# Combining expert outputs at the end of a mixture-of-experts stage: a selection product for the last expert, and the gathers of the others placed in the last round

## The chip, the cores and the metric

One core of a Trainium2 chip runs the whole program. The metric is the device time of one execution in microseconds. Three runs of the kernel before gave 1581.63, 1583.05 and 1589.31 us; their median is 1583.05 us.

## What is computed

The reference is a two-layer decoder over 512 tokens of width 1024. Layer 0 mixes tokens by an RWKV-7 recurrence, layer 1 by dilated window attention. Each layer ends with the same hierarchical mixture of experts: the router picks one of 4 groups and two of the 4 experts inside it, and the token's output is the weighted sum of the two:

```
gate = (one_hot(grp)[:, :, None] * within[:, None, :] * p_grp[:, :, None]).reshape(n_tok, 16)
y = zeros_like(t)
for e in range(16):
    hdn = silu(t @ w_gate[e]) * (t @ w_up[e])      # (1024 x 512) twice
    y = y + gate[:, e:e + 1] * (hdn @ w_down[e])   # (512 x 1024)
h = h + y
```

So only two of the 16 terms of a token differ from zero. A final RMS norm follows after layer 1.

## The kernel before

The stage is `moe(nc, io, g, layer)`, called once for each layer. P is 128 partitions, J = 4 is the number of tiles of 128 tokens, T = 512, D = 1024, NE = 16. The residual `h` is resident in SBUF as 128 x 4 x 1024. The stage does not multiply all tokens by all experts. Each expert has 128 places; a token of expert e with position `posf` there is in row 128 e + `posf` of that expert's block.

**Prologue.** VectorE (DVE) computes the router's choices, the weights `wgt` (one for each of the two choices), the position `posf` of every token within its expert, the list of tokens of each expert (`idx`) and, for each token and choice, the row of the DRAM buffer `out_dram` where its output will stand (`pos`). These are some 60 small DVE instructions, most of which wait for the one before (`Chain.link`). The last two write `most` and `mosti`, the length of the longest list (L1821, L1822). All 16 x 128 rows of `out_dram` that these places use are filled with zeros once, in the layer-0 mixing stage (L748).

**Rounds.** There is one round for each expert; the first and the last are written out, the 14 between are a hardware loop on each engine (`rounds`). SyncE loads each expert's three weight matrices in six 1 MB pieces (L1429). ScalarE (ACT) rounds each piece to a high part (L1435), DVE subtracts for the low part (L1439, or in two halves at L1830), and TensorE (PE) multiplies in three passes (L1446 to L1448). In round e, PE does gate half 0, the transposes of the hidden values of expert e-1 (`pe_hidden`, L1467), gate half 1, both halves of the down product of e-1, the transposes of the tokens of e+1 (`pe_tokens`, L1458), and both halves of up. ACT copies the two halves of the down product from PSUM to the one tile `yo` (L1527). After the last round (`moe` from `rounds(pe, round_)` on) PE still has the transposes and the down product of expert 15. DVE there does: the product gate x up (`dve_up`, L1509), one and a half of the last two splits, the low part of the hidden values (`dve_hidden`, L1519), and the other half split.

**GpSimd (POOL)** gathers the tokens of an expert (L1614, L1619) and stores its output: `store_output` copies a column of row numbers (L1530), waits for both halves of `yo`, issues an indirect DMA to `out_dram` (L1534), waits until it has landed and only then frees `yo`.

**End.** POOL waits for the last of the 16 stores, then issues 8 indirect gathers (L1651), for each token tile j its first and its second choice, 512 KB each, into the tiles `xn` and `xnT`. Between the wait and the gathers it makes four checks whether a list is longer than 128 (`overflow`, `no_overflow`: a value is loaded from SBUF to a register, then a branch). With such a list there would be further rounds. Only DVE adds: for each j it waits for both gathers of that tile, then makes two additions `h += wgt * row` of 128 x 1024 (L1878), each of which waits for the one before. ACT squares each finished tile of `h` for the next norm (`square_tile`, L63). Then all engines meet at a barrier (L96) and the next stage begins: attention after layer 0, the final norm and the store of the result after layer 1.

## Time and profile before

| | |
|---|---|
| median of three runs | 1583.05 us (1581.63 to 1589.31) |
| the profiled execution, own time | 1583.01 us |
| its span, first to last instruction | 1581.3 us |
| mean granted TensorE clock | 0.93 |
| busy: PE, PEld, DVE, ACT, POOL | 1360.4, 1066.0, 1006.1, 845.0, 373.4 us |
| expert stage of layer 0 | about 520 to 877 us in the span |
| expert stage of layer 1 | about 1213 to 1570 us |

Busy shares are means over stages with different limits. In the rounds PE is busy nearly all of the time; at the end of each expert stage it is not. Times in the timelines are microseconds from the start of the span, then the duration; the bracket at the end of a row gives how long the engine had been idle and what it waited for ("issue" is a time for which the profile names no releaser).

### The profile page before, as it was taken

How to read it: one execution, taken by the hardware profiler on the slowest of the kernel's cores; microseconds unless marked ns; L12 is line 12 of the kernel's file. 1: busy time of each engine (PE TensorE's matmuls, PEld its weight loads, DVE VectorE, ACT ScalarE, POOL GpSimd, SP SyncE). 2: the span in 40 equal slices, each digit the busy share in tenths (PEclk: the TensorE clock that was granted, in tenths of full speed). 3: DMA queues.
4: the chain of work that ended last, by engine and by line, in shares of the span. 5: the costliest groups of instructions: out<-in, count | busy, mean ns of one | idle time of the engine just before them, and what ended most of it. 6: DMA issues, size and time to landing. Idle time of an engine off the chain costs nothing. (4 is left out here: it accounts for less than half of the span.)

```text
span 1581.3 us, 29588 instructions
## 1 busy us (share of the span) xinstructions
PE 1360.4 (86%) x11579; PEld 1066.0 (67%) x11579; DVE 1006.1 (64%) x1316; ACT 845.0 (53%) x1255; POOL 373.4 (24%) x417
## 2 busy tenths in 40 slices
PE   4999996767689799999993599999988899999980
PEld 2276685657554678787882487778776778787860
DVE  5626752455643599989982435765444798989963
ACT  6535542434421378888881324444542488888851
POOL 1112153436440022332222100001110122332202
PEclk8999897998999799999996799999968899999995
DMA  5042300052442699999983331212102799999944
GB/s 167 20 140 80 133 1 15 16 153 84 136 149 94 221 347 380 379 384 382 379 325 115 115 121 55 80 54 80 54 1 89 285 379 383 383 385 376 377 165 167
DMA packets 172329, 302.46 MB, mean 191 GB/s; under 512 B 34720, under 2 KB 45088, under 8 KB 172224
## 3 DMA queue, kind: packets, MB, share of 16 engines
q1 hardware_dynamic: 159648, 271.59, 48.3%
q0 software_dynamic: 11520, 25.19, 4.3%
q10 hardware_dynamic: 1056, 4.19, 0.6%
q8 instruction: 76, 1.25, 0.3%
q14 instruction: 29, 0.24, 0.0%
HBM read 279.96 MB, written 35.65 MB: 200 GB/s over the span
## 5 line engine op out<-in xcount | busy, mean ns | idle before, releaser
L1439 DVE TENSOR_TENSOR moe_wlo<-moe_raw,moe_whi 128x2048 fp32r<-128x2048 f32 x160 | 365.4, 2287 | 36.4 <-ACT moe_whi L1435 32.0
L1435 ACT ACTIVATE moe_whi<-moe_raw 128x2048 fp32r<-128x2048 f32 x192 | 366.8, 1916 | 23.6 <-PE all_bank L1448 22.3
L1446 PE MATMUL all_bank<-moe_whi,moe_xhi 128*128 128x512 f32 x512 | 206.8, 404 | 4.1 <-DVE moe_xlo L1495 4.1
L1448 PE MATMUL all_bank<-moe_whi,moe_xlo 128*128 128x512 f32 x512 | 199.7, 390 | 0.0
L1447 PE MATMUL all_bank<-moe_wlo,moe_xhi 128*128 128x512 f32 x512 | 199.7, 390 | 0.0
L1446 PEld LDWEIGHTS all_bank<-moe_whi,moe_xhi 128*128 128x128 f32 x512 | 96.0, 187 | 26.7 <-DVE moe_xlo L1495 4.4
L1448 PEld LDWEIGHTS all_bank<-moe_whi,moe_xlo 128*128 128x128 f32 x512 | 96.1, 188 | 21.1
L1447 PEld LDWEIGHTS all_bank<-moe_wlo,moe_xhi 128*128 128x128 f32 x512 | 96.2, 188 | 18.1
L1446 PE MATMUL all_bank<-moe_whi,moe_hhi 128*128 128x512 f32 x256 | 101.9, 398 | 7.4 <-DVE moe_hlo L1519 7.4
L1611 POOL COPY moe_idxcol<-moe_idx 128x1 int32 (+1 forms) x30 | 34.5, 1150 | 310.9 <-PE all_bank L1458 310.9
L1447 PE MATMUL all_bank<-moe_wlo,moe_hhi 128*128 128x512 f32 x256 | 101.2, 395 | 0.0
L1448 PE MATMUL all_bank<-moe_whi,moe_hlo 128*128 128x512 f32 x256 | 101.1, 395 | 0.0
L2048 DVE SCALAR_TENSOR_TENSOR attn_wlo<-attn_xhat,all_par,attn_whi 128x512 fp32r<-128x512 f32 x64 | 43.8, 746 | 83.2 <-ACT attn_whi L2042 83.2
L2361 PE MATMUL all_bank<-attn_xhi,attn_whi 128*128 128x512 f32 x192 | 78.6, 410 | 6.5 <-DVE attn_xlo L2246 6.5
L900 ACT ACTIVATE chunks_pw<-all_bank 128x256 f32<-128x256 f32 x144 | 48.3, 387 | 62.3 <-PE all_bank L1241 41.8
L1830 DVE TENSOR_TENSOR moe_wlo<-moe_raw,moe_whi 128x1024 fp32r<-128x1024 f32 x64 | 77.8, 1215 | 0.0
L2362 PE MATMUL all_bank<-attn_xlo,attn_whi 128*128 128x512 f32 x192 | 76.8, 400 | 0.0
L2363 PE MATMUL all_bank<-attn_xhi,attn_wlo 128*128 128x512 f32 x192 | 76.6, 399 | 0.0
L1025 DVE TENSOR_TENSOR chunks_pw<-all_bank,chunks_pw 64x256 f32<-64x256 f32 x64 | 27.0, 422 | 66.9 <-PE all_bank L1249 65.5
L1446 PEld LDWEIGHTS all_bank<-moe_whi,moe_hhi 128*128 128x128 f32 x256 | 49.1, 192 | 18.7 <-issue 8.5
L237 DVE TENSOR_TENSOR project_wlo<-all_h,project_whi 128x2048 fp32r<-128x2048 f32 x12 | 29.6, 2467 | 49.0 <-ACT project_whi L233 49.0
L1530 POOL COPY moe_outcol<-moe_outidx 128x1 int32 (+1 forms) x32 | 53.7, 1679 | 28.7 <-DMA out_dram<-moe_yo,moe_outcol 28.7
(422 smaller groups left out, 2971.0 us busy)
## 6 DMA issues: line engine op xcount, KB each, us to landing
moe_raw<-in_moe_w_gate_dram SPq DMA_DIRECT2D x64, 1024.0 KB, 10.2
moe_raw<-in_moe_w_up_dram SPq DMA_DIRECT2D x64, 1024.0 KB, 9.5
moe_raw<-in_moe_w_down_dram SPq DMA_DIRECT2D x64, 1024.0 KB, 8.8
attn_xhat<-in_w_kv_dram SPq DMA_DIRECT2D x10, 1024.0 KB, 5.0
out_dram<-all_gain SPq DMA_DIRECT2D x16, 512.0 KB, 3.8
attn_xhat<-in_attn_w_q_dram SPq DMA_DIRECT2D x6, 1024.0 KB, 5.0
all_h<-in_rwkv_w_k_dram SPq DMA_DIRECT2D x4, 1024.0 KB, 9.1
all_h<-in_rwkv_w_v_dram SPq DMA_DIRECT2D x4, 1024.0 KB, 5.1
```

Source lines behind the costliest of these rows:

```text
L900: inc(nc.scalar.activation(dst, src, ACT.Copy), name)
L1435: nc.scalar.activation(whi[slot % SPLITS][:, :], raw[slot % 6][:, :], ACT.Copy).then_inc(m["hi_ok"], 1)
L1439: nc.vector.tensor_tensor(wlo[slot % SPLITS][:, :], raw[slot % 6][:, :], whi[slot % SPLITS][:, :].bitcast(fp32), ALU.subtract).then_inc(m[ ...
L1446: nc.tensor.matmul(bank[b][:, :], hi[:, k0 + k, :], wh[:, k, :], start=begin and k == 0, stop=False)
L1447: nc.tensor.matmul(bank[b][:, :], hi[:, k0 + k, :], wl[:, k, :], start=False, stop=False)
L1448: ins = nc.tensor.matmul(bank[b][:, :], lo[:, k0 + k, :], wh[:, k, :], start=False, stop=end and k == 3)
L1530: nc.gpsimd.tensor_copy(outcol[:, :], outidx[:, bass.ds(col, 1)]).then_inc(m["oc_ok"], 1)
L1830: ins = nc.vector.tensor_tensor(wlo[slot % SPLITS][:, cols], raw[slot % 6][:, cols], whi[slot % SPLITS][:, cols].bitcast(fp32), ALU.subtract)
L2048: ins = nc.vector.scalar_tensor_tensor(out=wlo[n % 2][:, k, :], in0=raw_of(n)[:, k, :], scalar=gain(n, k) if n < NP else 1.0, in1=whi[n % ...
L2361: nc.tensor.matmul(out, a[0], b[0], start=begin, stop=False)
L2362: nc.tensor.matmul(out, a[0], b[1], start=False, stop=False)
L2363: return nc.tensor.matmul(out, a[1], b[0], start=False, stop=end)
```

## The change

It concerns `moe` in both layers: the end of the DVE prologue, the last round and what stands behind it.

- The last expert's output is no longer stored. Its rows of `out_dram` keep what they held: zeros. In `yo` the 128 rows are multiplied with a selection matrix: `picks[t, j, r]` is 1 where token t of tile j has place r in the last expert (a DVE comparison in the last round, into the free half of `xg`), PE transposes it in the last round between the down product of expert 14 and the up product of expert 15 (four 128 x 128 transposes), ACT copies it to SBUF, and after both halves of `yo` are there, eight plain float32 products of 128 x 128 by 128 x 512 put each token's row into eight PSUM banks.
- DVE adds those with the weight `last_wgt`, eight 128 x 512 instructions, after the eight additions of the gathered rows.
- POOL waits for the store of expert 14 only and then issues the gathers at once; the checks for a long list come after them, on every engine, and what belongs to places of 128 and more is gathered and added in that branch. The gathers now have a bounds check.
- The prologue has seven more small DVE instructions, for `near`, `last_place` and `last_wgt`.
- In the last round DVE splits the first down piece ahead of `dve_up`, and the second one whole after `dve_hidden`.

```diff
@@ gpsimd
-            for e in range(NE - 3, NE):
+            for e in range(NE - 3, LASTE):
                 store_output(pool, main, e, e)
-            pool.wait_ge(pos_ok, 2)
-            with overflow(pool):
...
-            pool.wait_ge(main["y_st"], 16 * NE)
-            with overflow(pool):
-                pool.wait_ge(more["y_st"], 16 * NE * (J - 1))
 
             def outputs(rows):
                 for j in range(J):
                     for k in range(2):
                         dst = (xn if k == 0 else xnT2)[:, j, :]
-                        pool.indirect_dma_start(dst, None, rows, bass.IndirectOffsetOnAxis(ap=pos[:, k, j:j + 1], axis=0)).then_inc(comb_in[j], 16)
-
+                        pool.indirect_dma_start(dst, None, out_dram[0:rows, :], bass.IndirectOffsetOnAxis(ap=pos[:, k, j:j + 1], axis=0),
+                                                bounds_check=rows - 1, oob_is_err=False).then_inc(comb_in[j], 16)
+
+            pool.wait_ge(pos_ok, 2)
+            pool.wait_ge(main["y_st"], 16 * LASTE)
+            outputs(NE * P)
             with overflow(pool):
-                outputs(out_dram)
-            with no_overflow(pool):
-                outputs(out_dram[0:NE * P, :])
-            for j in range(J):
-                pool.wait_ge(comb_in[j], 32)
...
@@ scalar
+                else:
+                    act.wait_ge(pick_done, 1)
+                    nc.scalar.activation(picksT, bank[0][:, :].rearrange("p (j t) -> p j t", j=J), ACT.Copy).then_inc(pick_T, 1)
...
             for j in range(J):
-                act.wait_ge(comb_ok, 2 * j + 2)
+                act.wait_ge(last_ok, 2 * j + 2)
                 square_tile(nc, act, g, j, raw[0][:, 0:D], squared)
@@ vector
+            mine = [Mk[:, :, NG - 1, EG - 1] for Mk in (M1, M2)]
+            ch.inc(V.scalar_tensor_tensor(out=near[:, :, :], in0=posf[:, :, :], scalar=float(P), in1=wgt[:, :, :], op0=ALU.is_lt, op1=ALU.mult))
+            for k, out in enumerate((last_place, last_wgt)):
+                ch.inc(V.scalar_tensor_tensor(out=out[:, :], in0=posf[:, k, :], scalar=1.0, in1=mine[k], op0=ALU.add, op1=ALU.mult))
+            ch.wait()
+            ch.link(V.scalar_tensor_tensor(out=last_place[:, :], in0=last_place[:, :], scalar=-1.0, in1=last_wgt[:, :], op0=ALU.add, op1=ALU.add))
+            tt(last_wgt[:, :], mine[0], wgt[:, 0, :], ALU.mult)
+            tt(v4[6][:, :], mine[1], wgt[:, 1, :], ALU.mult)
+            tt(last_wgt[:, :], last_wgt[:, :], v4[6][:, :], ALU.add)
...
+                if last:
+                    dve.wait_ge(main["xt_done"], NE + 1)
+                    V.tensor_tensor(picks, g["iota"].rearrange("p (x r) -> p x r", x=1).to_broadcast([P, J, P]),
+                                    last_place[:, :].rearrange("p (j x) -> p j x", x=1).to_broadcast([P, J, P]), ALU.is_equal).then_inc(pick_ok, 1)
+                    split_lo(dve, main, *then(0))
+                    dve_up(dve, main, e, piece(e, x, 5)[0])
+                    return
...
             rounds(dve, round_)
             dve_hidden(dve, main, NE - 1)
-            part_lo(*piece(NE, 0, 1)[:2], 1)
+            split_lo(dve, main, *piece(NE, 0, 1)[:2])
+            combine(near, 1, comb_ok)
+            for j in range(J):
+                for half in range(2):
+                    dve.wait_ge(last_mm, 2 * j + half + 1)
+                    hh = h[:, j, 512 * half:512 * half + 512]
+                    V.scalar_tensor_tensor(out=hh, in0=last_bank(j, half)[:, :], scalar=last_wgt[:, j:j + 1], in1=hh, op0=ALU.mult, op1=ALU.add).then_inc(last_ok, 1)
@@ tensor
+                else:
+                    pe.wait_ge(pick_ok, 1)
+                    pe.wait_ge(main["xl_ok"], 2 * NE + 1)
+                    for j in range(J):
+                        ins = nc.tensor.transpose(bank[0][:, P * j:P * j + P], picks[:, j, :], g["ident"][:, :])
+                    ins.then_inc(pick_done, 1)
...
+            pe.wait_ge(main["y_ok"], 2 * NE + 1)
+            pe.wait_ge(pick_T, 1)
+            for j in range(J):
+                for half in range(2):
+                    nc.tensor.matmul(last_bank(j, half)[:, :], picksT[:, j, :], yo[:, 512 * half:512 * half + 512], start=True, stop=True).then_inc(last_mm, 1)
```

`combine(weights, taken, done)` is the loop of L1878 as it was: for each j it waits for `32 * taken` on `comb_in[j]`, then makes two additions of 128 x 1024, with the weights `near` in place of `wgt`.

## Rows read from the trace of the kernel before

**Rows 1.** Timeline of ACT, end of layer 1's expert stage.
```profile
1540.74 0.60 ACT L1527 ACTIVATE moe_yo<-all_bank 128x512 f32<-128x512 f32 x1 [2.14 <-PE all_bank L1448]
...
1567.93 1.06 ACT L63 ACTIVATE moe_raw<-all_h 128x1024 f32<-128x1024 f32 x1 [1.49 <-DVE all_h L1878]
1570.35 1.28 ACT L2511 ACT_TABLE_LOAD   x1 [1.27 <-PEq L96]
```
**Rows 2.** Timeline of POOL, end of layer 1's expert stage.
```profile
1524.17 0.98 POOL L1534 DMA_INDIRECT out_dram<-moe_yo,moe_outcol  x1 [9.87 <-ACT moe_yo L1527]
1527.53 0.18 POOL L1530 COPY moe_outcol<-moe_outidx 128x1 int32<-128x1 int32 x1 [2.38 <-DMA out_dram<-moe_yo,moe_outcol]
1542.18 0.98 POOL L1534 DMA_INDIRECT out_dram<-moe_yo,moe_outcol  x1 [14.46 <-ACT moe_yo L1527]
1549.40 0.99 POOL L1651 DMA_INDIRECT moe_xn<-out_dram,moe_pos  x1 [6.24 <-issue]
...
1556.93 1.59 POOL L1651 DMA_INDIRECT moe_xn<-out_dram,moe_pos  x1 [0.30 <-issue]
1558.82 1.01 POOL L1651 DMA_INDIRECT moe_xnT<-out_dram,moe_pos  x1 [0.30 <-issue]
```
**Rows 3.** Timeline of DVE, end of layer 1's expert stage.
```profile
1519.72 2.29 DVE L1439 TENSOR_TENSOR moe_wlo<-moe_raw,moe_whi 128x2048 fp32r<-128x2048 f32 x1 [0.34 <-ACT moe_whi L1435]
1528.17 0.69 DVE L1509 TENSOR_TENSOR moe_hid<-all_bank,moe_sg 128x512 f32<-128x512 f32 x1 [6.15 <-PE all_bank L1448]
...
1532.11 0.74 DVE L1519 TENSOR_TENSOR moe_hlo<-all_bank,moe_hhi 128x256 fp32r<-128x256 f32 x2
...
1556.42 1.28 DVE L1878 SCALAR_TENSOR_TENSOR all_h<-moe_xn,moe_wgt,all_h 128x1024 f32<-128x1024 f32 x1 [22.43 <-DMA moe_xnT<-out_dram,moe_pos]
...
1560.01 1.28 DVE L1878 SCALAR_TENSOR_TENSOR all_h<-moe_xn,moe_wgt,all_h 128x1024 f32<-128x1024 f32 x1 [0.99 <-DMA moe_xnT<-out_dram,moe_pos]
...
1566.61 1.28 DVE L1878 SCALAR_TENSOR_TENSOR all_h<-moe_xnT,moe_wgt,all_h 128x1024 f32<-128x1024 f32 x1
```
**Rows 4.** The same end in layer 0, timelines of POOL and then DVE.
```profile
834.30 0.18 POOL L1530 COPY moe_outcol<-moe_outidx 128x1 int32<-128x1 int32 x1 [2.40 <-DMA out_dram<-moe_yo,moe_outcol]
...
856.48 0.99 POOL L1651 DMA_INDIRECT moe_xn<-out_dram,moe_pos  x1 [6.44 <-issue]
...
873.14 1.28 DVE L1878 SCALAR_TENSOR_TENSOR all_h<-moe_xnT,moe_wgt,all_h 128x1024 f32<-128x1024 f32 x1
```
**Rows 5.** Windows: length; busy PE, PEld, DVE, ACT, POOL; clock; DMA share; GB/s.
```profile
1528.20:1533.00 4.80, 0.50 (x9) 0.42 (x9) 4.80 (x6) 0.66 (x2) 0.00 (x0) 0.73 0.01 2
1541.00:1542.00 1.00, 0.00 (x0) 0.00 (x0) 0.00 (x0) 0.33 (x1) 0.00 (x0) 1.00 0.00 0
1560.00:1562.60 2.60, 0.00 (x0) 0.00 (x0) 2.56 (x2) 0.20 (x2) 0.00 (x0) 0.50 1.03 418
```
**Rows 6.** Timeline of PE: float32 products at L1279, transposes at L1894.
```profile
503.64 1.88 PE L1279 MATMUL all_bank<-rwkv_rw_w,rwkv_rw_k 128*128 128x512 f32 x4
505.36 1.88 PE L1279 MATMUL all_bank<-rwkv_rw_xT,rwkv_rw_k 128*128 128x512 f32 x4
...
522.81 5.68 PE L1894 MATMUL all_bank<-all_ident,moe_xn 128*128 128x128 f32 x32
```
**Rows 7.** Timeline of DVE: the first additions at L1071, layer 0's mixing stage.
```profile
484.97 1.29 DVE L1071 TENSOR_TENSOR all_h<-all_bank,all_h 128x512 f32<-128x512 f32 x2 [6.41 <-DMA all_h<-in_x_dram]
```
**Rows 8.** Timeline of DVE, end of layer 1's prologue.
```profile
1256.03 0.16 DVE L1738 TENSOR_REDUCE moe_most<-moe_v 128x1 f32<-128x16 f32 x1
1256.22 0.15 DVE L1822 CAST moe_mosti<-moe_most 128x1 int32<-128x1 f32 x1
1256.97 2.29 DVE L1439 TENSOR_TENSOR moe_wlo<-moe_raw,moe_whi 128x2048 fp32r<-128x2048 f32 x1 [0.60 <-ACT moe_whi L1435]
```
**Rows 9.** Waits in layer 0's second round, the last that names PE.
```profile
PE all_bank L1446 <- DVE moe_hlo L1519: 0.3, 1, 0.3
```
**Rows 10.** DMA issues of the page: stores of the experts' outputs, with KB and landing.
```profile
out_dram<-moe_yo,moe_outcol POOLq DMA_INDIRECT x32, 6.8
```

More of the change, by code:

```diff
@@ L1633, in _ @@
                 pool.wait_ge(main["xt_done"], NE + 1)
+                pool.wait_ge(last_mm, 2 * J)
                 pool.wait_ge(idx_ok, 2)
@@ L1641, in _ @@
                 each_further(pool, further_round)
[L1643 to L1644 removed]
                 pool.wait_ge(more["y_st"], 16 * NE * (J - 1))
[L1647 to L1658 removed]
+                pool.wait_ge(comb_ok, 2 * J)
+                outputs(NE * T)
         @block.scalar
@@ L1873, in _ @@
                 each_further(dve, further_round)
-            for j in range(J):
-                dve.wait_ge(comb_in[j], 32)
-                for k in range(2):
-                    src = (xn if k == 0 else xnT2)[:, j, :]
-                    V.scalar_tensor_tensor(out=h[:, j, :], in0=src, scalar=wgt[:, k, j:j + 1], in1=h[:, j, :], op0=ALU.mult, op1=ALU.add).then_inc(comb_ok, 1)
-                    dve.wait_ge(comb_ok, 2 * j + k + 1)
+                ch.link(V.scalar_tensor_tensor(out=near[:, :, :], in0=posf[:, :, :], scalar=float(P), in1=wgt[:, :, :], op0=ALU.is_ge, op1=ALU.mult))
+                dve.wait_ge(last_ok, 2 * J)
+                combine(near, 2, late_ok)
         @block.tensor
```

36 lines of the change are left out of this document (23 added, 13 removed).

## The prediction

> **What bounds the kernel now.** I read the timelines of the four engines over the end of an expert stage first, then the windows for clock and DMA, then the waits in the rounds. In the rounds PE is busy without gaps. After them a chain begins in which each link waits for the one before. In layer 1: ACT writes the second half of the last `yo` until 1541.34 [rows 1]; POOL issues the last store at 1542.18 and the first gather at 1549.40; six gathers on, the seventh is issued at 1556.93, so they follow each other by 1.25 us, and the eighth comes 1.89 behind it, beside DVE's additions [rows 2]. DVE starts at 1556.42, waits once more for 0.99, and from 1560.01 on never waits: its eight additions, each 1.32 behind the last (1.28 and 0.04 of semaphore), end at 1567.89 [rows 3]. ACT's last square starts 0.04 later, and the next stage's first ACT instruction comes at 1570.35 [rows 1]. Nothing of PE or of the weight loads stands in these 29 us. Layer 0 has the same chain, from the first gather at 856.48 to an end at 874.42 [rows 4]. What any edit here is worth is how far it moves the end of DVE's last addition to `h`; what follows it is unchanged.
>
> **When the gathers start.** The new condition is that the store of expert 14 has landed. That store is issued at 1524.17, and the copy behind it, which waits for exactly this landing, runs at 1527.53 [rows 2]. In layer 0 that copy is at 834.30 [rows 4]. The checks between wait and gather are gone. If the last store lands as fast as that of expert 14 (3.36 from issue to copy), it lands at 1545.54, and 3.86 of the 7.22 us to the first gather [rows 2] are the four checks, about 0.97 each. I take the first gather 0.3 after the time of the copy, the gap ahead of a gather that follows another [rows 2]: 1527.8 and 834.6. Bounds: 0 after it, or the whole 3.86 if the pause isn't the checks (a rival below). The store of expert 14 itself doesn't move: the new ACT copy and the PE transposes stand behind the second half of its `yo`.
>
> **From there to the end of the eight additions.** The same eight gathers and the same eight additions took 1567.89 less 1549.40 = 18.5 us in layer 1 [rows 2, 3] and 874.42 less 856.48 = 17.9 in layer 0 [rows 4]. DMA was nearly empty before them in both versions, since the last weights are in SBUF by then (0.01 of the engines in the window before the old down product [rows 5]). The new thing is that DVE works beside the first gathers: 0.69 for gate x up, 0.74 for the low part of the hidden values, 2.28 for a whole split. Gathers beside DVE's additions took 1.59 in place of 0.99 [rows 2]. One or two more of the eight would meet this, and the store of expert 14 may overlap the moved split: I add 0.5 us (from 0, if the transfers set the pace anyway, to 8 x 0.64 = 5.1, if each one does: a rival). The transfers do set the pace at 1560 to 1562.6, where all DMA engines are busy, at 418 GB/s [rows 5]. The Trainium skill (SBUF — State Buffer, "Who interferes with whom") says that a DVE instruction with two SBUF inputs contends with a GpSimd instruction that reads SBUF, and infers that making descriptors needs only the write side, so the stretch should be none; the row with 1.59 speaks for some, and by that page the sum would be 0.5 us a layer lower.
>
> DVE must be free when the first pair has landed, 7.0 after the first gather, at 1534.8. Its work before that: `dve_up` follows PE by the same 0.4 as now. PE starts the up product later, since it waits for the comparison (after the split that ends at 1522.01, 0.69 as another 128x512 comparison or product, so 1522.8 with its semaphore, against 1522.5 when PE is ready) and makes 4 transposes at 5.68 / 32 = 0.18 [rows 6]; with the pauses of a change of operands about 1.1 us. The split moved ahead of `dve_up` lies in an idle time of 6.15 [rows 3]. So `dve_up` is at 1529.3, the hidden transposes and ACT's copy follow as before until about 1531.2, DVE's low part ends at 1531.8 in place of 1532.85 (no split is ahead of it any more), and the whole split ends at 1534.1. That is just in time; a slip of a few tenths goes into the range. The eight additions end at 1527.8 + 18.5 + 0.5 = 1546.8; in layer 0 at 834.6 + 17.9 + 0.5 = 853.0.
>
> **The selection products** are not the bound. The down product of expert 15 started behind DVE's low part (1532.85 [rows 3]), after the clock had fallen to 1.2 GHz within 1528.2 to 1533 (mean 0.73, PE idle but for 0.50 [rows 5]), and ended at 1540.7, when ACT took its second half [rows 1]. It now starts about 1.0 earlier; at the same two clocks it ends at 1539.7, and `yo` is complete at 1540.3. A float32 product of 128x512 stands as two records 0.43 apart (1.72 from one group of four to the next [rows 6]), so 0.86 each at full clock, and the clock is 1.00 in the us after the down product [rows 5]: eight take 6.9, the first is there at 1541.3, the last at 1547.3. DVE comes to its first one at 1546.8 and to its eighth some 4 us later.
>
> **The eight further additions** of 128x512, one operand in PSUM, are on the path whole. The nearest rows: two unweighted additions of this shape from PSUM in 1.29, which with 0.69 for one product from PSUM [rows 3] is 0.60 apart [rows 7]; the weighted ones at L1878, from SBUF, take 1.28 for 1024 columns and 0.04 of semaphore, so 0.64 to 0.68 for 512 [rows 3]. Bounds 7 x 0.60 + 0.69 = 4.9 and 8 x 0.68 = 5.4; I take 5.2, since the semaphores are reached long before. ACT's squares (1.06 and a short read of the sum [rows 1]) keep up with two additions a tile, about 1.3, so the last square again starts 0.04 after DVE's end. DVE's check for a long list (0.97) runs beside the last square and is just covered.
>
> So `h` is finished at 1546.8 + 5.2 = 1552.0 in place of 1567.9: 15.9 us less. Layer 0: 853.0 + 5.2 = 858.2 in place of 874.4: 16.2 less.
>
> **The prologue.** Seven more DVE instructions stand ahead of the first round's splits: four linked ones at 0.2 (0.19 from one such to the next at the end of the prologue [rows 8]) and three that don't wait for each other, which can't cost more than that and for which I take 0.1: 1.1 to 1.2 in all. DVE then waited 0.60 for ACT [rows 8], which covers half; 0.6 is left. In the second round PE waits 0.3 for DVE's low part of the hidden values [rows 9] and has no slack afterwards, so 0.6 us passes to PE and to the rest of the layer. Bounds 0 and 1.2. Two layers: 1.2. Everything else (the comparison, ACT's copy, ahead of a rounding that DVE now needs only at 1531.8, the allocations) costs nothing on this path.
>
> **Sum:** 15.9 + 16.2 - 1.2 = 30.9 us less. The profiled execution took 1583.01 (span 1581.3), the median is 1583.05, so both give 1552.1.
>
> **Rivals.**
> A: the pause before the first gather isn't the four checks but belongs to the first gather, which the profile calls only "issue" [rows 2]. Then the gathers start at 1531.4, 3.6 later than in the sum: 1552.1 + 7.2 = 1559.3. For it: no row shows a check by itself. Against: a gather after a gather pauses 0.30, and four value loads must cost something.
> B: the gathers are stretched by DVE throughout, 0.64 each. The second gather of the first pair was there 5.8 after its issue (1556.42 less 1550.65), so the eighth at about 1564.6. All 21.6 earlier and 5.1 later is 1548.1, its two additions end at 1550.7 in place of 1546.8: 3.9 more a layer, 1559.9. Against: only the gathers beside additions show it, not their neighbours.
> C: TensorE stays at 1.2 GHz for the selection products: 8 x 1.72 = 13.8, the last at 1554.2, DVE's end at 1554.9, 2.9 more a layer: 1557.9. Against: 1.00 behind the same down product [rows 5].
> D, on the slow side: DVE and POOL exclude each other. Each pair of gathers then waits for the additions of the pair before, and the chain is serial: 2.5 for two issues, 4.8 until they have landed, 2.6 for two additions, four times: 39.6 in place of 19.0, 20.6 more a layer, 1593.3. It decides from the point where the chain is over 34.9 us long. The Trainium skill's same section tells of such a case, a DMA issued from GpSimd of 0.62 us that took 3.1 beside a DVE copy; with 3.1 for each gather the eight would be issued over 27 us in place of 10, and by that estimate the time would be about 1586. Against D: two gathers were issued in the midst of the additions at 1556.9 and 1558.8 and lost 0.6 [rows 2].
> E: the change doesn't do what it says, as it would with a list longer than 128. The trace has 32 stores, 16 a layer, and none of further rounds [rows 10], so the branch isn't taken.
>
> **How the numbers follow.** Forecast 0.70, A 0.12, B 0.08, C 0.05, D 0.03, and 0.02 for no change. The range goes down by 1.0 (no stretch), 0.6 (the lower bound of the additions) and 1.2 (a prologue at no cost) to 1549.3, and with some tenths for a gather straight behind the landing to 1548; up it takes in C, A and B: 1560. A difference of under 0.5%, 7.9 us, is what a measurement of this kernel can't tell from none. Faster by more than that 0.95, within it 0.02, slower 0.03.
>
> **What would show it.** Right: the first gather within 1 us of the landing of expert 14's store; DVE idle only a little between the last split and the first addition; eight additions of 128x512 at 0.6 to 0.7 directly behind the others, without a wait on PE; the last square 28 us after the store of expert 14 is issued, where it was 43.8 (1567.93 less 1524.17). Wrong: a pause of 4 us ahead of the first gather (A), gathers over 1.5 us apart throughout (B), a clock of 0.50 in the selection products (C), additions that alternate with gathers (D), or PE waiting for the selection comparison for over a microsecond.

## The result: 1.5 per cent faster, seven tenths of the gain that was forecast

| | before | after |
|---|---|---|
| median | 1583.70 us (four runs, 1581.63 to 1589.31) | 1561.91 us (four runs, 1559.26 to 1563.46) |
| ratio, with its 95% interval | | 0.9855 [0.9833, 0.9876] |
| profiled execution | 1583.01 us, span 1581.3 | 1562.04 us, span 1560.3 |
| mean granted TensorE clock | 0.930 | 0.941 |
| store of expert 14 issued until `h` finished, layer 0 | 43.5 us | 31.3 us |
| the same, layer 1 | 43.7 us | 31.0 us |

The fifth and sixth rows start at the store of expert 14, the last one that both kernels have. The forecast was 1552.1 us, 30.9 less than before; the profiled execution was 21.0 less, the median 21.8, and both lie above the upper end of the range, 1560. The mechanism is there: gathers, additions and selection products run beside the down product of expert 15. One stretch of it is 2 to 3 us a layer longer than forecast.

The timeline of POOL in the kernel after, two of layer 0's gathers and then the end of layer 1 without two gathers of usual length (start, duration, engine and line, operation; in the bracket how long the engine had been idle and on whom it waited):

```profile
840.54 2.91 POOL L1637 DMA_INDIRECT moe_xn<-out_dram,moe_pos  x1 [0.30 <-issue]
...
845.05 1.64 POOL L1637 DMA_INDIRECT moe_xn<-out_dram,moe_pos  x1 [0.30 <-issue]
...
1515.90 1.50 POOL L1539 DMA_INDIRECT out_dram<-moe_yo,moe_outcol  x1 [9.87 <-ACT moe_yo L1532]
1520.57 1.04 POOL L1637 DMA_INDIRECT moe_xn<-out_dram,moe_pos  x1 [3.17 <-DMA out_dram<-moe_yo,moe_outcol]
1521.92 1.01 POOL L1637 DMA_INDIRECT moe_xnT<-out_dram,moe_pos  x1 [0.31 <-issue]
1523.23 2.91 POOL L1637 DMA_INDIRECT moe_xn<-out_dram,moe_pos  x1 [0.30 <-issue]
1526.44 0.99 POOL L1637 DMA_INDIRECT moe_xnT<-out_dram,moe_pos  x1 [0.30 <-issue]
1527.74 1.54 POOL L1637 DMA_INDIRECT moe_xn<-out_dram,moe_pos  x1 [0.30 <-issue]
...
1532.20 1.78 POOL L1637 DMA_INDIRECT moe_xnT<-out_dram,moe_pos  x1 [0.30 <-issue]
```

Read against [rows 2]: the store of expert 14 took 0.98 before and takes 1.50. The first gather follows it by 4.67, where it followed the last store by 7.22. The third gather takes 2.91, the fifth 1.54, the eighth 1.78; the others stay at 0.99 to 1.04. From the first gather's start to the eighth's end it is 13.4 us in place of 10.4. Layer 0 shows the same.

The timeline of DVE in the same kernel, layer 1:

```profile
1514.26 2.29 DVE L1444 TENSOR_TENSOR moe_wlo<-moe_raw,moe_whi 128x2048 fp32r<-128x2048 f32 x1
1520.57 0.69 DVE L1514 TENSOR_TENSOR moe_hid<-all_bank,moe_sg 128x512 f32<-128x512 f32 x1 [4.02 <-PE all_bank L1453]
1522.32 0.76 DVE L1524 TENSOR_TENSOR moe_hlo<-all_bank,moe_hhi 128x256 fp32r<-128x256 f32 x2 [1.06 <-ACT moe_hhi L1519]
1522.99 2.28 DVE L1444 TENSOR_TENSOR moe_wlo<-moe_raw,moe_whi 128x2048 fp32r<-128x2048 f32 x1
1527.13 1.28 DVE L1874 SCALAR_TENSOR_TENSOR all_h<-moe_xn,moe_near,all_h 128x1024 f32<-128x1024 f32 x1 [1.85 <-DMA moe_xnT<-out_dram,moe_pos]
1528.45 1.29 DVE L1874 SCALAR_TENSOR_TENSOR all_h<-moe_xnT,moe_near,all_h 128x1024 f32<-128x1024 f32 x1
1531.84 1.28 DVE L1874 SCALAR_TENSOR_TENSOR all_h<-moe_xn,moe_near,all_h 128x1024 f32<-128x1024 f32 x1 [2.10 <-DMA moe_xnT<-out_dram,moe_pos]
1533.15 1.28 DVE L1874 SCALAR_TENSOR_TENSOR all_h<-moe_xnT,moe_near,all_h 128x1024 f32<-128x1024 f32 x1
...
1538.92 1.29 DVE L1874 SCALAR_TENSOR_TENSOR all_h<-moe_xn,moe_near,all_h 128x1024 f32<-128x1024 f32 x1 [1.05 <-DMA moe_xnT<-out_dram,moe_pos]
...
1541.57 5.36 DVE L1885 SCALAR_TENSOR_TENSOR all_h<-all_bank,moe_last_wgt,all_h 128x512 f32<-128x512 f32 x8
```

Two things are to be seen. First, DVE waits for a pair of gathers four times (1.85, 2.10, 0.83 in a row left out, 1.05), where before it waited twice and then never [rows 3]. Second, lay the two timelines side by side. The third gather is issued at 1523.23; the split of 1522.99 ends at 1525.27, 2.04 later, and the gather 0.87 behind that. The fifth, issued at 1527.74, has 0.67 until the addition of 1527.13 ends at 1528.41, and 0.87 behind it. The eighth, issued at 1532.20, has 0.92 until the addition of 1531.84 ends at 1533.12 and 0.86 behind it. The store of expert 14, issued at 1515.90, has 0.65 until the split of 1514.26 ends and 0.85 behind it. The theory from this: **an indirect DMA's issue that meets a running DVE instruction stands until that instruction ends, and only then takes its 0.87 us.** It fits [rows 2, 3] as well, with 0.82 in place of 0.87: the gather of 1.59 at 1556.93 had 0.77 until the addition of 1556.42 ended. (A gather alone takes 0.93 to 0.96 there and 0.99 here; the bounds check is the difference between the two that the diff shows, and no run has it by itself.)

A split holds an issue in the kernel before, too. These are a store in the last rounds of layer 1 and DVE's row beside it, in the trace of before:

```profile
1506.37 1.40 POOL L1534 DMA_INDIRECT out_dram<-moe_yo,moe_outcol  x1 [4.76 <-ACT moe_yo L1527]
1504.62 2.29 DVE L1439 TENSOR_TENSOR moe_wlo<-moe_raw,moe_whi 128x2048 fp32r<-128x2048 f32 x1 [0.43 <-ACT moe_whi L1435]
```

The store has 0.54 until the split ends and 0.86 behind it; the store of 1524.17 in [rows 2], beside which DVE is idle, takes 0.98.

What the long third gather does to the transfers stands in the windows of the same kernel (length; busy PE, PEld, DVE, ACT, POOL; clock; DMA share; GB/s):

```profile
1523.20:1525.20 2.00, 2.00 (x5) 1.61 (x6) 2.00 (x1) 0.00 (x0) 1.97 (x1) 0.50 0.92 340
1525.20:1527.20 2.00, 2.00 (x8) 1.57 (x7) 0.14 (x2) 0.00 (x0) 1.70 (x2) 0.72 0.60 168
```

With two gathers in flight the DMA engines are busy; then they run low for 2 us, 168 GB/s, until the third and fourth are issued. Work that is held up here can't be won back where the transfers themselves set the pace later.

ACT and PE of the same kernel at the end of layer 1; first ACT:

```profile
1530.41 0.60 ACT L1532 ACTIVATE moe_yo<-all_bank 128x512 f32<-128x512 f32 x1 [2.12 <-PE all_bank L1453]
...
1546.96 1.06 ACT L63 ACTIVATE moe_raw<-all_h 128x1024 f32<-128x1024 f32 x1 [0.17 <-DVE all_h L1885]
...
1549.41 1.28 ACT L2551 ACT_TABLE_LOAD   x1 [1.30 <-PEq L96]
```

and PE's eight selection products:

```profile
1531.06 7.13 PE L1978 MATMUL all_bank<-moe_yo,moe_xg 128*128 128x512 f32 x16 [0.69 <-ACT moe_yo L1532]
```

`yo` is complete at 1531.0 and the products end at 1538.2, 3.4 us before DVE comes to the first of them. The last square starts 0.03 after DVE's last addition, as in [rows 1], and the next stage's table load 2.45 later, where it was 2.42.

### The profile page after: what moved, and what is told of

Its sections match the earlier page's. It is cut to its first block and busy times, and to the rows that moved or that the text cites. A ratio compares the mean times of both kernels' runs of the same rounds, so it can differ in the third digit from the quotient of the medians.

```text
span 1560.3 us, 29684 instructions
## 1 busy us (share of the span) xinstructions
PE 1380.5 (88%) x11619; PEld 1077.1 (69%) x11619; DVE 1020.5 (65%) x1346; ACT 846.2 (54%) x1257; POOL 377.5 (24%) x413
## 5 line engine op out<-in xcount | busy, mean ns | idle before, releaser
L1444 DVE TENSOR_TENSOR moe_wlo<-moe_raw,moe_whi 128x2048 fp32r<-128x2048 f32 x162 | 370.2, 2288 | 35.1 <-ACT moe_whi L1440 30.7
L1842 DVE TENSOR_TENSOR moe_wlo<-moe_raw,moe_whi 128x1024 fp32r<-128x1024 f32 x60 | 73.1, 1218 | 0.0
```

Source lines behind the costliest of these rows:

```text
L1444: nc.vector.tensor_tensor(wlo[slot % SPLITS][:, :], raw[slot % 6][:, :], whi[slot % SPLITS][:, :].bitcast(fp32), ALU.subtract).then_inc(m[ ...
L1842: ins = nc.vector.tensor_tensor(wlo[slot % SPLITS][:, cols], raw[slot % 6][:, cols], whi[slot % SPLITS][:, cols].bitcast(fp32), ALU.subtract)
```

## The experiments

The first three ask whether the hold is real and what causes it, the next four whether the rest of the gain is where the prediction put it. All are edits of the kernel after, but for the one that says otherwise.

**The split out of the gathers' way.** The second of the last two splits is made ahead of gate x up, so that none is left beside the gathers:

```diff
                     split_lo(dve, main, *then(0))
+                    split_lo(dve, main, *then(1))
                     dve_up(dve, main, e, piece(e, x, 5)[0])
                     return
...
             dve_hidden(dve, main, NE - 1)
-            split_lo(dve, main, *piece(NE, 0, 1)[:2])
             combine(near, 1, comb_ok)
```

> The kernel after with the second down split placed ahead of the product gate x up, where DVE is idle from 1516.6 to 1520.6 in the trace of after. Theory 1 (a gather's issue stands still until the DVE instruction with two SBUF inputs that is running has ended): the third gather no longer meets a split, takes 1.0 in place of 2.91 us, the eight issues take about 11.5 in place of 13.4 us, and DVE's last addition of a gathered row ends about 1.5 to 1.9 us a layer earlier: 3 to 4 us less in all, about 1558. Theory 2 (the gathers are slower because of the bounds check or because TensorE and ACT are at work): the third gather stays at 2 us or more or another takes its place, and the time doesn't move.

Measured: 1557.73 us, as expected; ratio to the kernel before 0.984 [0.9809, 0.9872]. Its POOL, layer 1:

```profile
1508.87 1.50 POOL L1539 DMA_INDIRECT out_dram<-moe_yo,moe_outcol  x1 [9.87 <-ACT moe_yo L1532]
1513.54 1.04 POOL L1637 DMA_INDIRECT moe_xn<-out_dram,moe_pos  x1 [3.17 <-DMA out_dram<-moe_yo,moe_outcol]
...
1516.20 0.99 POOL L1637 DMA_INDIRECT moe_xn<-out_dram,moe_pos  x1 [0.30 <-issue]
...
1522.67 0.99 POOL L1637 DMA_INDIRECT moe_xnT<-out_dram,moe_pos  x1 [0.30 <-issue]
```

its DVE:

```profile
1510.51 2.29 DVE L1444 TENSOR_TENSOR moe_wlo<-moe_raw,moe_whi 128x2048 fp32r<-128x2048 f32 x1 [0.98 <-ACT moe_whi L1440]
...
1520.17 1.28 DVE L1875 SCALAR_TENSOR_TENSOR all_h<-moe_xn,moe_near,all_h 128x1024 f32<-128x1024 f32 x1 [4.14 <-DMA moe_xnT<-out_dram,moe_pos]
...
1532.04 5.36 DVE L1885 SCALAR_TENSOR_TENSOR all_h<-all_bank,moe_last_wgt,all_h 128x512 f32<-128x512 f32 x8
```

The third gather is back at 0.99, the eight are issued in 10.1 us, and from the first gather to the end of the eight additions it is 18.5 us (18.0 in layer 0), which are the very numbers of the kernel before (18.5 and 17.9) that the prediction had used. The store of expert 14 is still 1.50, since it still meets a split. In the window that answers to the thin one above, DMA doesn't run low:

```profile
1518.20:1520.20 2.00, 2.00 (x8) 1.54 (x8) 0.03 (x1) 0.00 (x0) 1.39 (x3) 0.74 0.94 346
```

**Which DVE instructions hold an issue.** In the next kernel the four weighted additions of tile 0 read an operand of 128 x 512 from PSUM, in place of the gathered rows in SBUF. The output leaves out the gathered rows of tile 0; the selection products of tiles 2 and 3 wait for those additions.

```diff
+                        if j == 0 and taken == 1:
+                            if k == 0:
+                                dve.wait_ge(pick_T, 1)
+                            V.scalar_tensor_tensor(out=h[:, j, 0:512], in0=bank[0][:, :], scalar=weights[:, k, j:j + 1], in1=h[:, j, 0:512], op0=ALU.mult, op1=ALU.add)
+                            V.scalar_tensor_tensor(out=h[:, j, 512:1024], in0=bank[0][:, :], scalar=weights[:, k, j:j + 1], in1=h[:, j, 512:1024], op0=ALU.mult, op1=ALU.add).then_inc(done, 1)
+                        else:
+                            V.scalar_tensor_tensor(out=h[:, j, :], in0=src, scalar=weights[:, k, j:j + 1], in1=h[:, j, :], op0=ALU.mult, op1=ALU.add).then_inc(done, 1)
...
             for j in range(J):
+                if j == 2:
+                    pe.wait_ge(comb_ok, 2)
                 for half in range(2):
```

> The kernel after, but the additions of tile 0 read a PSUM bank in place of the gathered rows, as four instructions of 128x512 with one SBUF input, so the gathered rows of tile 0 are left out of the sum. Theory 1 (two SBUF inputs hold the issue up): the fifth gather, which met the first addition and took 1.54 us, takes 1.0; the third, beside the split, stays at about 2.9; the gathers after the fifth come 0.5 us earlier. Theory 2 (any DVE work holds it up, or none does): the fifth stays at 1.5, or varies without regard to what DVE runs. The time moves by 0 to 1 us a layer.

Measured: 1561.76 us, one run. Its POOL and then its DVE in layer 1:

```profile
1522.39 2.93 POOL L1637 DMA_INDIRECT moe_xn<-out_dram,moe_pos  x1 [0.30 <-issue]
...
1526.92 1.00 POOL L1637 DMA_INDIRECT moe_xn<-out_dram,moe_pos  x1 [0.30 <-issue]
```

```profile
1526.61 0.75 DVE L1877 SCALAR_TENSOR_TENSOR all_h<-all_bank,moe_near,all_h 128x512 f32<-128x512 f32 x1 [2.15 <-DMA moe_xnT<-out_dram,moe_pos]
1527.27 0.74 DVE L1878 SCALAR_TENSOR_TENSOR all_h<-all_bank,moe_near,all_h 128x512 f32<-128x512 f32 x1
```

The fifth gather is issued in the midst of the first of these additions and takes 1.00, where it took 1.54 beside the addition from SBUF. The third, beside the unchanged split, still takes 2.93. Three more gathers of this run meet such an addition with 0.23 to 0.58 of it left and take 0.99. The rounds say the same: over all traces of this study 338 stores are issued in the midst of gate x up, which has one operand in PSUM, with 0.25 to 0.29 of it left, and take 1.01 to 1.04. A hold would make them 1.11 and more, an estimate from the 0.86 behind each end. So what holds is the DVE instruction with both inputs in SBUF. The instructions from PSUM are also narrower, 512 columns or fewer against 1024 and 2048, and no run separates the two. The second lesson is in the time: the eight gathers were issued over 12.0 us, 1.3 less than in the kernel after, and the chain of gathers and additions was not shorter (20.7 and 21.5 us a layer, against 21.2 and 21.0). The hold on the third gather is thus the one that costs: at that point few transfers are queued, while behind it the transfers set the pace (in the kernel after the DMA engines are busy for 0.92 to 1.01 of the time from 1529.2 to 1535.2) and cover a later issue.

**The order of before.** DVE's work of the last round put back in its old order: gate x up, a whole split, half a split, the low part, half a split.

```diff
-                    split_lo(dve, main, *then(0))
                     dve_up(dve, main, e, piece(e, x, 5)[0])
+                    split_lo(dve, main, *then(0))
+                    part_lo(*then(1), 0)
                     return
...
-            split_lo(dve, main, *piece(NE, 0, 1)[:2])
+            part_lo(*piece(NE, 0, 1)[:2], 1)
```

> The kernel after with DVE's splits of the last round in the order of the kernel before (product gate x up, one and a half splits, low part of the hidden values, half a split). Theory 1 gives each gather: the store of expert 14 meets no split and takes 0.98 in place of 1.50; the first gather comes 4.1 to 4.2 after it in place of 4.67; the second gather meets the whole split and ends 0.87 after it, at 2.5 to 3.2 us; a later one meets a half split. DVE's last split ends about 3 us later than the first pair's landing would need in split_early, so DVE and gathers end together: 0 to 1.5 us a layer later than the kernel after. Theory 2 (DVE doesn't matter): all gathers near 1.0 to 1.5.

Measured: 1558.36 us, one run. POOL, layer 1, and then DVE:

```profile
1513.04 0.98 POOL L1539 DMA_INDIRECT out_dram<-moe_yo,moe_outcol  x1 [9.87 <-ACT moe_yo L1532]
...
1518.54 2.93 POOL L1637 DMA_INDIRECT moe_xnT<-out_dram,moe_pos  x1 [0.31 <-issue]
...
1523.07 1.30 POOL L1637 DMA_INDIRECT moe_xnT<-out_dram,moe_pos  x1 [0.30 <-issue]
...
1528.87 1.93 POOL L1637 DMA_INDIRECT moe_xnT<-out_dram,moe_pos  x1 [0.30 <-issue]
```

```profile
1518.30 2.28 DVE L1444 TENSOR_TENSOR moe_wlo<-moe_raw,moe_whi 128x2048 fp32r<-128x2048 f32 x1
1520.50 1.22 DVE L1842 TENSOR_TENSOR moe_wlo<-moe_raw,moe_whi 128x1024 fp32r<-128x1024 f32 x1
...
1522.30 1.21 DVE L1842 TENSOR_TENSOR moe_wlo<-moe_raw,moe_whi 128x1024 fp32r<-128x1024 f32 x1
...
1528.64 1.29 DVE L1875 SCALAR_TENSOR_TENSOR all_h<-moe_xn,moe_near,all_h 128x1024 f32<-128x1024 f32 x1 [0.95 <-DMA moe_xnT<-out_dram,moe_pos]
```

The hold moves with the splits: the store of expert 14 is free again (0.98), the second gather is now the one of 2.93 (2.04 until the split of 1518.30 ends, 0.89 behind it), the fourth has 0.44 of the half split of 1522.30 and 0.86, the eighth 1.06 of an addition and 0.87. The half split that starts at 1520.50 follows the whole one at once and doesn't hold the second gather any longer. The chain took 19.9 and 20.7 us. The loss of 0 to 1.5 us a layer that had been expected didn't come: the chains are 1.3 and 0.3 shorter than in the kernel after. They are longer than with the early split, so this order is no cure either.

**Selection product without the early gathers.** POOL waits for the eight selection products before it gathers:

```diff
             pool.wait_ge(main["y_st"], 16 * LASTE)
+            pool.wait_ge(last_mm, 2 * J)
             outputs(NE * P)
```

> The kernel after with the gathers issued only when all eight selection products are done, so at 1538 in place of 1520.6 in layer 1. They then meet no split, only additions. Theory 1: the chain from first gather to the end of the eight additions is again 18 to 18.6 us as in the kernel before, in place of 21.0; so the time rises by 17.5 less 2.5, 15 us a layer, to about 1592: the selection product without early gathers is slower than the kernel before. Theory 2 (the bounds check makes the gathers slow): the chain stays at 21 us, and the time is about 1597.

Measured: 1588.01 us, ratio 1.0029 [1.0011, 1.0048]; the first gather comes 23.3 us after the store of expert 14, and the chain behind it takes 18.4 and 17.8 us, without a split beside it. One gather of layer 1 is long:

```profile
1549.60 1.04 POOL L1637 DMA_INDIRECT moe_xn<-out_dram,moe_pos  x1 [21.80 <-PE all_bank L1979]
...
1557.44 1.17 POOL L1637 DMA_INDIRECT moe_xn<-out_dram,moe_pos  x1 [0.30 <-issue]
```

```profile
1556.46 1.28 DVE L1875 SCALAR_TENSOR_TENSOR all_h<-moe_xn,moe_near,all_h 128x1024 f32<-128x1024 f32 x1 [20.78 <-DMA moe_xnT<-out_dram,moe_pos]
```

Even the small number fits: 0.30 until the addition of 1556.46 ends and 0.87 behind it. The time is 4 us below the 1592 that had been expected; the stretch from the store of expert 14 to the finished `h` is 15.8 and 15.4 us longer than in the kernel after, 31.3 in all, and the medians differ by 26.1, so the rest is in parts that the edit doesn't touch. The selection product with the gathers behind it is therefore a small loss against the kernel before, although the checks are out of the way too. What brings the gain is that the gathers of the other experts may start a round earlier.

**The four checks of the kernel before.** This one is an edit of the kernel before: further rounds and both branches on the list's length are taken out of POOL's program, and with them the four value loads. It computes the case of lists up to 128 alone.

```diff
-            with overflow(pool):
-                start(pool, more, ["col_ok", "oc_ok"])
...
             pool.wait_ge(main["y_st"], 16 * NE)
-            with overflow(pool):
-                pool.wait_ge(more["y_st"], 16 * NE * (J - 1))
...
-            with overflow(pool):
-                outputs(out_dram)
-            with no_overflow(pool):
-                outputs(out_dram[0:NE * P, :])
+            outputs(out_dram[0:NE * P, :])
```

> The kernel before without POOL's four checks for a long list and the further rounds on POOL; the lists of these inputs are short, so nothing that is computed changes. If the 3.9 us between the landing of the last store and the first gather are the four checks (the prediction's view), the first gather comes 3.2 to 3.6 us after the landing's earlier place, the time falls by 3.3 to 3.9 us a layer, 7 us in all, to about 1576.5. Rival A of the prediction (the pause belongs to the first gather): no change, 1583.7.

Measured: 1574.71 us, ratio 0.9947 [0.9928, 0.9966]. POOL, layer 1:

```profile
1542.97 0.98 POOL L1534 DMA_INDIRECT out_dram<-moe_yo,moe_outcol  x1 [14.40 <-ACT moe_yo L1527]
1547.07 0.99 POOL L1638 DMA_INDIRECT moe_xn<-out_dram,moe_pos  x1 [3.12 <-DMA out_dram<-moe_yo,moe_outcol]
```

From the last store's issue to the first gather it is 4.10 in place of the 7.22 of [rows 2], so the four checks cost 3.1 us a layer and rival A is out. The median is 8.6 us below that of the kernel before (5.4 to 11.4 by the interval), where the rows give 6.2. That is a part of the 21.8 us for which no selection product is needed. A kernel that only moves the checks behind the gathers, and keeps the case of long lists, wasn't run. The gather itself begins 3.12 after the end of the store's issue, where the copy of [rows 2] began 2.38 after it: straight behind a wait a gather starts 0.7 us later than the copy, not 0.3.

**The products doubled.** Each of the eight selection products is made twice:

```diff
+                    nc.tensor.matmul(last_bank(j, half)[:, :], picksT[:, j, :], yo[:, 512 * half:512 * half + 512], start=True, stop=True)
                     nc.tensor.matmul(last_bank(j, half)[:, :], picksT[:, j, :], yo[:, 512 * half:512 * half + 512], start=True, stop=True).then_inc(last_mm, 1)
```

> The kernel after with each of the eight selection products made twice (same result), 6.9 us more of TensorE. In the trace of after they end at 1538.2 and DVE comes to the first at 1541.6 and to the eighth at 1546.3. If DVE with the gathers sets the end (theory 1), the products end at about 1545.1 and DVE's last further addition at 1546.9 as before: 0 to 0.3 us a layer. If TensorE were what bounds the end, the time would rise by 6.9 a layer.

Measured: 1558.19 us, one run, as expected no more than the kernel after. PE's last doubled product and DVE's row behind it, layer 1:

```profile
1539.62 1.02 PE L1979 MATMUL all_bank<-moe_yo,moe_xg 128*128 128x512 f32 x2
```

```profile
1537.70 5.36 DVE L1885 SCALAR_TENSOR_TENSOR all_h<-all_bank,moe_last_wgt,all_h 128x512 f32<-128x512 f32 x8
```

The eight additions still take 5.36 without a wait, although the products now end at 1540.6, 6.9 later than single ones would. TensorE has slack, and a clock of 1.2 GHz (rival C, the same doubling) would have cost nothing.

**Small instructions out of the prologue.** `near` and the three instructions of `last_wgt` moved from the prologue into the last round, ahead of gate x up:

```diff
-            ch.inc(V.scalar_tensor_tensor(out=near[:, :, :], in0=posf[:, :, :], scalar=float(P), in1=wgt[:, :, :], op0=ALU.is_lt, op1=ALU.mult))
...
-            tt(last_wgt[:, :], mine[0], wgt[:, 0, :], ALU.mult)
-            tt(v4[6][:, :], mine[1], wgt[:, 1, :], ALU.mult)
-            tt(last_wgt[:, :], last_wgt[:, :], v4[6][:, :], ALU.add)
...
                     split_lo(dve, main, *then(0))
+                    ch.inc(V.scalar_tensor_tensor(out=near[:, :, :], in0=posf[:, :, :], scalar=float(P), in1=wgt[:, :, :], op0=ALU.is_lt, op1=ALU.mult))
+                    tt(last_wgt[:, :], mine[0], wgt[:, 0, :], ALU.mult)
+                    tt(v4[6][:, :], mine[1], wgt[:, 1, :], ALU.mult)
+                    tt(last_wgt[:, :], last_wgt[:, :], v4[6][:, :], ALU.add)
                     dve_up(dve, main, e, piece(e, x, 5)[0])
```

> The kernel after with four of the seven small prologue instructions (the weights) moved to the last round, where DVE is idle. From the second copy of a token list to the store of expert 14 the kernels with all seven have taken 268.5 to 269.4 us and those without 268.6 to 268.9. If the prediction's 0.6 a layer was right, this kernel is back at 268.7 or below in both layers; if the small ones were hidden, it stays at the same 269.1 on average. One look can't tell less than 0.4.

Measured: 1558.37 us, one run. In the stretch that the expectation names, from POOL's second copy of a token list to the store of expert 14, it takes 269.04 us in layer 1 and 268.75 in layer 0, so it isn't down to 268.7. Layer 1 has an order (268.63 and 268.68 without the seven, 269.03 to 269.05 with three of them, 269.25 to 269.46 with all seven and early gathers), layer 0 has none, between 268.54 and 269.19. The stretch from the first copy, which also holds the end of the prologue, is clearer. It has a shortest form that comes back to within some hundredths:

| | shortest form, us | stretches that have it | the others |
|---|---|---|---|
| none of the seven (before, without checks) | 277.43 to 277.46 | 3 of 4 | 279.01 |
| all seven in the prologue | 277.86 to 277.92 | 11 of 16 | 279.0 to 280.4 |
| three of them (this run, both runs of the next kernel) | 277.49 to 277.50 | 4 of 6 | 278.9 |

So the seven cost 0.45 us a layer, of which the four that moved give 0.4 back. What makes a stretch 1.1 to 2.5 us longer isn't known; it occurs without the seven, too.

**Both edits**, the split ahead of gate x up and the four small instructions late, in one kernel.

> The kernel after with the second down split ahead of the product gate x up and, between the two down splits of the last round (DVE idle there for 0.98 us), four of the seven small instructions of the prologue. Expected if each part is worth what its own rows say: the end as in split_early (18.5 us from first gather to the end of the eight additions, every gather near 1.0 us), and the stage 0.3 to 0.6 us shorter a layer from the second token list's copy to the store of expert 14: 4 to 5 us less than the kernel after, about 1557. If the small instructions cost nothing on the path, it equals split_early.

Measured: 1552.53 us, ratio 0.9803 [0.9788, 0.9817]: the lowest median of the study. Its profiled execution, at 1558.58, was the longest of its five. One gather of its layer 1 goes against the theory as it was put above; POOL and DVE:

```profile
1526.11 0.99 POOL L1637 DMA_INDIRECT moe_xnT<-out_dram,moe_pos  x1 [0.30 <-issue]
1526.06 1.30 DVE L1875 SCALAR_TENSOR_TENSOR all_h<-moe_xn,moe_near,all_h 128x1024 f32<-128x1024 f32 x1 [3.99 <-DMA moe_xnT<-out_dram,moe_pos]
```

The gather is issued 0.05 after the addition has begun and isn't held. Over all traces of the study 91 issues meet a DVE instruction with two SBUF inputs that has run for 0.16 or more and has 0.17 or more left. All of them end 0.81 to 0.89 behind it. With 0.13 or less left a gather takes its usual 0.99 or 1.00.

**The three versions side by side.** Since the ratios above come from different chips, the kernel after, the early split and both edits were run again on one chip, beside nine runs of the kernel before (1583.27 us).

> The changed kernel once more, beside the two versions that differ from it on the same chip, to separate the lock from the run-to-run spread of TensorE's clock. Lock theory: the store of expert 14 at 1.50 us and the third gather at 2.9 us in both layers again, since instructions of fixed length meet there; store to first gather 4.67; first gather to the end of the eight additions 20 to 21.5 us. If 2.7 us of my miss were clock of this one execution, the start of stage and the 32 transposes come out otherwise here (between 4.7 and 6.7 us) and the time lies at 1557 to 1562. Rival: the long gather came from what was on the chip then; then it is gone or elsewhere.

> Only the second split moved ahead of gate x up. Lock theory: no gather over 1.2 us, chain 18 to 18.5 us a layer, in place of 20 to 21.5, so 4 to 5 us below the changed kernel on the same chip: about 1554 to 1557. Rival (the time is set by the transfers, the gathers' pace is nothing): same as the changed kernel within 1 us.

> The split early and four small instructions late. If the small instructions in the prologue cost 0.6 us a layer, 1 us below the split alone; if they cost nothing, the same within 0.5 us. Against the changed kernel on the same chip: 4 to 7 us less. No gather over 1.2 us. The chain of layer 0, which took 19.6 us at the first look though no gather was long, tells by its waits what else can stretch it.

| | median, us | ratio to before | first gather to end of eight additions, layers 0 and 1 |
|---|---|---|---|
| after | 1560.89 | 0.9864 [0.9844, 0.9883] | 21.0, 21.2 |
| split early | 1557.13 | 0.9848 [0.9820, 0.9876] | 18.6, 18.4 |
| both | 1555.95 | 0.9830 [0.9814, 0.9846] | 18.1, 18.1 |

The third gather of the kernel after is 2.93 and 2.94 us again, the store 1.50: the hold belongs to the program and not to one execution. The early split is 3.8 us below the kernel after, where its chains are 2.4 and 2.8 shorter, 5.2 in all; the intervals of the two overlap, so its gain rests on the chains more than on the medians. Both edits together are 4.9 below, and the intervals hardly overlap. The chain of 19.6 us in layer 0 that the first profiled execution of both edits had shown was 18.1 here. There DVE had waited 1.40 us for the last pair, in a kernel whose gathers were all issued in 10.4 us, so the transfers were late and not their issues; what slowed them isn't known.

## Why the prediction was wrong in size and right in kind

The profiled execution is 9.9 us above the forecast. By the prediction's own steps:

**From there to the end of the eight additions** is the step that failed. The prediction took 17.9 and 18.5 us from the trace and added 0.5 for DVE's work beside the gathers. Measured were 21.2 and 21.0: 2.8 and 2.0 us over, 4.8 together. It had seen both rows that matter, the gather of 1.59 beside an addition and the whole split that moves beside the gathers, and had read the first as a stretch of 0.64 for any gather that meets DVE. It is a hold, as long as what is left of the DVE instruction: 0.77 for an addition that had run for 0.5, 2.04 for a split of 2.28 that had just begun. Moving the split out of the way gives the time back, as the early split shows. The price of a split could have been read before: the store of 1506.37 in the kernel before took 1.40 beside one. Rival B had the right place and the wrong price: it spread 0.64 over all eight gathers and so came out near the measured time, at 1559.9, by a sum that no row bears out.

The Trainium skill (SBUF — State Buffer, "Who interferes with whom") says that a DVE instruction with two SBUF inputs contends with a GpSimd instruction that reads SBUF, and the page's "Summary: rules for kernel authors" that the second of the two to be issued blocks fully until the first ends. With POOL as the second that is what the rows show, 0.81 to 0.89 us behind each end, and a gather beside PSUM operands is free (1.00), as the Trainium skill has it. With DVE as the second the rows don't show it: the addition of 1527.13, begun in the midst of a gather's issue, takes 1.28 like any other. The Trainium skill's section "Who interferes with whom" also infers that making descriptors needs only the write interface, so that such a DVE instruction wouldn't hold a DMA's issue; the prediction weighed that and put the sum only 0.5 above it. Here the measurement decides against the inference. That the indirect DMA reads its row numbers from SBUF would reconcile the two, but no run tests it.

**When the gathers start** was short by 1.0 us a layer: 4.67 after the store's issue where 3.66 were forecast. 0.52 of it is the hold of the store of expert 14 by the moved split, a case that the prediction names and puts into the same 0.5. The rest is the first gather's own beginning, 0.8 behind the time of the copy in place of 0.3. That the pause was the checks was right: 3.1 us of 7.2, where 3.86 had been put down to them.

**The eight further additions** were 5.40 from the last addition's end, against 5.2 (bounds 4.9 and 5.4): right, with 0.2 a layer over. The end of the last square, 0.03 behind DVE, was right.

**The selection products** were right. From the store of expert 14's issue the forecast had `yo` complete 16.1 us later and the last product 23.1 later; measured were 15.1 and 22.3. The last split ends 9.4 after that issue, forecast 9.9, so DVE was ready before the first pair. All of that was off the path, as forecast, and the doubled products show by how much.

These terms make 4.0 us in layer 0 and 3.2 in layer 1, 7.2 of the 9.9.

**The prologue and everything called unchanged** hold the other 2.8. Outside the stretches from the store of expert 14 to the finished `h` the profiled execution of after is 4.0 us longer than that of before, where 1.2 had been forecast. The seven small instructions are 0.9 of it, 0.45 a layer against the forecast 0.6: about right. The largest parts are the beginnings of the two expert stages up to the second token list, 1.7 each, in code that the change doesn't touch. Windows of 4 us at the same place, the 32 transposes of layer 1; the kernel after:

```profile
1206.90:1210.90 4.00, 4.00 (x21) 4.00 (x20) 2.93 (x3) 0.00 (x0) 0.00 (x0) 0.50 1.05 408
```

and the kernel with tile 0 from PSUM, whose prologue is the same:

```profile
1207.90:1211.90 4.00, 4.00 (x29) 4.00 (x27) 3.10 (x4) 0.24 (x1) 0.00 (x0) 0.72 1.03 390
```

The same work runs at 1.2 GHz (0.50) throughout in the one, and the clock has risen on the way in the other; the transposes take 6.62 and 5.04 us. Over all profiled executions they took 4.66 to 6.67 us, 4.66 and 6.61 in layer 0 of two executions of the kernel after. So the forecast carried one execution's clock into another's. How much such things make shows over all profiled executions: outside those stretches they take 1492.6 to 1498.7 us, the kernel before 1494.0, and the kernel before without checks, whose prologue is the same, 1497.5. The medians say that it isn't one execution's luck alone: they differ by 21.8 us, and by 22.4 when the kernel after was measured again, where the stretches give 24.9. Whether the edit has a part in it is open: in layer 1 nine of the ten executions with early gathers have the long form, and one of the three others.

Of the rivals A is out by the kernel without checks, C by the doubled products and by the 7.13 us of the eight at a granted clock of 1.00 (at 1.2 GHz they would be 13.8, the prediction's own estimate), and E because the trace has 30 stores, 15 a layer, and none of further rounds. D is out too, but it was nearer than it looked: POOL does wait for DVE, fully. It doesn't go the other way: the addition of 1527.13 starts in the midst of the fourth gather's issue and takes 1.28 like any other. The hold is seen in one direction only, and thus never becomes the serial chain of D. The case of 0.62 and 3.1 us that D quotes stands in the Trainium skill (SBUF — State Buffer, "A bandwidth-pool intuition that's wrong (but worth ruling out)"); it is of a DVE copy, which no run here has beside a gather.

## What to carry to other kernels

When a gather is moved beside other work, lay the two timelines together and ask of every DVE instruction with both inputs in SBUF how long it is, not how often it meets a gather: a hold is as long as the rest of that instruction. Keep the long ones out of the first gathers, when few transfers are queued; behind those a hold was covered here. And before a whole stage's gain is credited to an edit, try its parts: the selection product with late gathers lost 0.3 per cent, the kernel before gained 0.5 by losing its checks alone, and the 1.5 per cent came with the earlier start, which has the checks out of its way too.

## What the runs showed of the hardware that was not expected

- An indirect DMA's issue on POOL stands until the running DVE instruction with two SBUF inputs ends, and ends 0.81 to 0.89 us behind it (91 issues): 2.91 us beside a split of 2.28, against 0.99 alone. One issue that came 0.05 us after such an instruction had begun wasn't held (0.99). A DVE instruction that starts 0.04 us or less after the one that held it doesn't hold it again.
- An instruction of DVE with one operand in PSUM and 512 columns doesn't hold it: 1.00 us beside an addition from PSUM, 1.54 beside the wider one from SBUF.
- DVE isn't held by a gather's issue that it meets: 1.28 us for the addition in either case.
- A gather straight behind a wait for a DMA begins 0.7 to 0.8 us later than a small copy does (3.12 and 3.17 against 2.38 after the end of the store's issue), while one gather follows another by 0.30.
- Four value loads with their branches cost POOL 3.1 us, about 0.8 each.
